# Norm scales applied at the eviction from PSUM instead of before the matmul, in a layer of retention, spatial gating and MLP

## The reference, cut to what matters

```python
def rmsnorm(x, g):
    y = x * lax.rsqrt(jnp.mean(x * x, axis=-1, keepdims=True) + EPS)
    return y * g
...
z = rmsnorm(x, g_mix) @ w_in                     # (B,S,3072)
q, k, v, g, u, sv = split(z)                     # 512 columns each
q = rotary(q); k = rotary(k) * 128 ** -0.5
r = layernorm_nogain(chunk_retention(q, k, v))   # over each head's 128 columns
y_ret = silu(g) * r * ret_norm_g
y_sg = spatial_gating(gelu(u), gelu(sv), w_s, b_s, sg_norm_g)
x = x + concatenate([y_ret, y_sg]) @ w_out
x = x + square(relu(rmsnorm(x, g_ffn) @ w_ff1)) @ w_ff2
x = x + sigmoid(rmsnorm(x, g_ple) @ w_ple_gate) * (p @ w_ple)
return rmsnorm(x, g_final)
```

## Time and profile before

| | us |
|---|---|
| median of 3 runs (lowest, highest) | 3551.35 (3355.66, 3689.61) |
| the profiled execution, device time | 3347.36 |
| its span on the slowest core (core 4) | 3345.5 |
| spans of the 8 cores | 3313.2 to 3345.5 |
| PE busy, core 4 | 3107.9 (93%) |
| DVE, ACT, POOL busy, core 4 | 1844.7, 1166.7, 547.4 |

### The profile page before, as it was taken

How to read it: one execution, slowest core, us unless ns; L and a number is a source line. 1 busy time by engine, 2 the same in 40 slices (tenths; PEclk the granted TensorE clock), 3 DMA queues, 4 the chain that set the end, 5 groups by cost and what they waited for, 6 DMA issues and landing times.

```text
span 3345.5 us, 45255 instructions; the slowest of 8 cores (3313.2 to 3345.5 us)
## 1 busy us (share of the span) xinstructions
PE 3107.9 (93%) x15322; PEld 1451.9 (43%) x15628; DVE 1844.7 (55%) x2864; ACT 1166.7 (35%) x2153; POOL 547.4 (16%) x512
## 2 busy tenths in 40 slices
PE   5999999889989899898999999999899999999996
PEld 2434444334434344344444444444444444444442
DVE  6756556555455454554546556465655555565426
ACT  5543344323323333233333323333333333333322
POOL 3401101202022120210202212021221202111000
PEclk9879999999999999999999999999999999999998
DMA  8856566444646447464464645536464464645442
GB/s 271 245 175 190 185 211 218 145 132 140 209 127 199 135 136 210 127 199 132 133 215 153 194 141 163 199 125 213 140 198 152 144 214 135 199 128 177 151 151 82
DMA packets 110689, 568.16 MB, mean 170 GB/s; under 512 B 19064, under 2 KB 19192, under 8 KB 60288
## 3 DMA queue, kind: packets, MB, share of 16 engines
q1 hardware_dynamic: 95488, 551.51, 50.6%
q10 hardware_dynamic: 14976, 13.74, 3.4%
HBM read 504.28 MB, written 60.92 MB: 169 GB/s over the span
## 4 chain that ended last, share of the span: by engine, by line
PE 75%; DMA 11%; DVE 8%; issue 3%; ACT 1%; POOL 1%; SPq 0%; DVEq 0%; ACTq 0%; POOLq 0%
PE ps L638 72%; DMA rsB<-rsd 7%; DVE TG L733 4%; DMA rsd<-st 4%; DVE xb L1112 1%; DMA xb<-wf 1%; ACT sq L669 1%; PE ps L646 1%; DVE xb L1050 1%; PE ps L999 0%; SPq L518 0%; POOL st L695 0%; DVE sq L674 0%; PE ps L848 0%; PE ps L878 0%
## 5 line engine op out<-in xcount | busy, mean ns | idle before, releaser
L638 PE MATMUL ps<-TG,ring 128*128 128x512 bf16 x7537 | 1759.3, 389 | 151.9 <-DVE TG L733 134.1
L638 PEld LDWEIGHTS ps<-TG,ring 128*128 128x128 bf16 x7680 | 758.3, 100 | 1076.7 <-issue 267.1
L638 PE MATMUL ps<-hT,ring 128*128 128x512 bf16 x3980 | 911.4, 380 | 8.4 <-ACT ring L602 1.6
L638 PEld LDWEIGHTS ps<-hT,ring 128*128 128x128 bf16 x4096 | 395.5, 98 | 460.6 <-issue 15.8
L1029 ACT ACTIVATE rel<-ps 128x512 f32<-128x512 f32 x512 | 304.0, 595 | 651.5 <-PE ps L638 584.9
L669 ACT ACTIVATE sq<-xb 128x1024 bf16<-128x1024 f32 x256 | 270.0, 1055 | 558.8 <-DVE xb L1050 191.9
L1031 DVE TENSOR_TENSOR hT<-rel 128x512 bf16<-128x512 f32 x326 | 245.2, 756 | 287.7 <-ACT rel L1029 287.6
L638 PE MATMUL ps<-ring,TG 128*128 128x512 bf16 x1502 | 361.7, 384 | 8.1 <-ACT ring L602 4.4
L733 DVE TENSOR_TENSOR TG<-xb,rsB 128x1024 bf16<-128x1024 f32 x191 | 226.6, 1248 | 210.9 <-DMA rsB<-rsd 205.6
L1050 DVE TENSOR_TENSOR xb<-xb,ps 128x512 f32<-128x512 f32 x288 | 192.8, 682 | 143.1 <-PE ps L638 125.9
L695 POOL TENSOR_TENSOR st<-st,NEGH 128x4 f32<-128x4 f32 x64 | 65.4, 1022 | 1209.6 <-DVE st L692 1209.6
(11 more groups left out here) (101 smaller groups left out, 2053.7 us busy)
## 6 DMA issues: line engine op xcount, KB each, us to landing
ring<-wb SPq DMA_DIRECT2D x366, 1024.0 KB, 6.0
xb<-wf SPq DMA_DIRECT2D x104, 512.0 KB, 8.3
xb<-xT SPq DMA_DIRECT2D x64, 512.0 KB, 9.1
out<-xb SPq DMA_DIRECT2D x64, 512.0 KB, 5.0
wb<-ring SPq DMA_DIRECT2D x26, 1024.0 KB, 9.8
rsB<-rsd ACTq DMA_DIRECT2D x52, 256.0 KB, 6.1
xb<-pT SPq DMA_DIRECT2D x16, 512.0 KB, 10.8
rot<-ROT SPq DMA_DIRECT2D x15, 512.0 KB, 7.9
```

The costliest lines, as they stand in the source:

```text
L638: r = e.matmul(out(), lhs(k), rhs(k), start=(start + k == 0), stop=(start + k == total - 1))
```

## The change

The matmuls no longer read a normalized residual, but a plain bf16 cast of it (`cast`: four casts of 128x1024, on ACT or DVE as the model picks). A norm's scale is one number per token, so it can be applied to the result. `norm` (the former `rstd`) computes it beside the matmuls:

- q and k are left without a scale. That of q is one factor per token of the retention's result and falls out in its layernorm, whose eps is scaled to match (`EPSQ`, L919 before); that of k moves to v, which is multiplied with the squared scale and the decay `KD` as it leaves PSUM (always DVE, a 128x16 table in `st`). `ktok` becomes a plain copy (DVE or ACT), and the table `DTm` is divided by KD.
- g: tanh with the scale as ACT's per-partition scale, and once more in the last product of the retention. sv: gelu with a per-partition scale.
- u and gate: one more DVE operation, PSUM times `rsB`, then ACT's gelu or tanh reads SBUF.
- `f_up`: one DVE operation, max(PSUM, 0) times `rsB`, in place of ACT's relu; the square is then on ACT or POOL, no longer on DVE.
- In every tile the scale is spread by PE, in three bf16 parts instead of two (two more small DVE operations, 12 rows instead of 8). The DMAs over DRAM and the tensor `rsd` are gone. In tiles 0 and 1, for the norms of mixer and MLP, PE also sums the squares directly, 8 one-column matmuls for each square, in place of DVE's additions.
- The model's numbers: completion delays, DMA bandwidth, durations; four `rsB` slots instead of two, seven `scr` instead of nine.
- The start: the pieces of tile 0 and of weight q are loaded alternately, tile 1 behind them, and the first `wb` writes later.

```diff
-SEM_LAT = {"pe": 0.25, "act": 0.12, "dve": 0.12, "pool": 0.15, "sp": 0.05}
+SEM_LAT = {"pe": 0.30, "act": 0.12, "dve": 0.19, "pool": 0.17, "sp": 0.05}
...
-            dma(lambda: rs_d[idx], lambda: stc(st, 4, 4), [(st, "rs")], [(dr, 0)], vt, lambda: ("rw", st.slot), 0, q="act")
-            dma(lambda: ap(rb), lambda: rs_d[idx].rearrange("(o p) b -> o (p b)", o=1).partition_broadcast(128).rearrange(
-                "p o n -> p (o n)"), [(dr, 0)], [(rb, 0)], vt, lambda: ("rb", rb.slot), 0, q="act")
...
-                f = lambda e, j=j: e.tensor_tensor(out=ap(dst)[:, 2 * j:2 * j + 2, :], in0=ap(X[t][j]),
-                                                   in1=r()[:, None, :].to_broadcast([128, 2, TT]), op=ALU.mult)
+        def cast(t, vt):
             dst = g.buf("TG")
             for j in range(4):
+                g.add(both(1024, lambda e, j=j: e.tensor_copy(out=ap(dst)[:, 2 * j:2 * j + 2, :], in_=ap(X[t][j])),
+                           lambda e, j=j: e.activation(out=ap(dst)[:, 2 * j:2 * j + 2, :], in_=ap(X[t][j]), func=AF.Copy)),
+                      [(X[t][j], 0), (X[t][j], 1)], [(dst, j)], vt, lock=("dve",))
...
-                g.add(both(512, lambda e, o=o, p=p: e.tensor_copy(out=ap(o), in_=ps(p)),
-                           lambda e, o=o, p=p: e.activation(out=ap(o), in_=ps(p), func=AF.Copy), mode=1),
-                      [(p, 0)], [(o, 0)], vt.v)
+                g.add({"dve": (T512, lambda e, o=o, p=p, b=b: e.tensor_tensor(
+                    out=ap(o).rearrange("p (h d) -> p h d", h=4), in0=ps(p).rearrange("p (h d) -> p h d", h=4),
+                    in1=stc(m.st, 16 + 4 * b, 4)[:, :, None].to_broadcast([128, 4, 128]), op=ALU.mult))},
+                      [(p, 0), (m.st, "r2")], [(o, 0)], vt.v)
...
-            g.add({"act": (t_act(512), lambda e: e.activation(out=ap(r), in_=ps(p), func=AF.Relu))},
-                  [(p, 0)], [(r, 0)], vt.v)
+            g.add({"dve": (T512 + .05, lambda e: e.scalar_tensor_tensor(out=ap(r), in0=ps(p), scalar=0.0, in1=ap(rb),
+                                                                       op0=ALU.max, op1=ALU.mult))},
+                  [(p, 0), (rb, 0)], [(r, 0)], vt.v)
+            g.add({"act": (t_act(512), lambda e: e.activation(out=ap(o), in_=ap(r), func=AF.Square)),
+                   "pool": (1.1, lambda e: e.tensor_tensor(out=ap(o), in0=ap(r), in1=ap(r), op=ALU.mult))},
+                  [(r, 0)], [(o, 0)], vt.v, lock=("pool",))
...
-                g.add({"act": (t_act(512), lambda e, p=p, gt=gt: e.activation(out=ap(gt), in_=ps(p), func=AF.Tanh,
-                                                                            scale=0.5))},
-                      [(p, 0)], [(gt, 0)], vt.v)
+                g.add({"dve": (T512, lambda e, p=p, gt=gt: e.tensor_tensor(out=ap(gt), in0=ps(p), in1=ap(rb), op=ALU.mult))},
+                      [(p, 0), (rb, 0)], [(gt, 0)], vt.v)
+                g.add({"act": (t_act(512), lambda e, gt=gt: e.activation(out=ap(gt), in_=ap(gt), func=AF.Tanh, scale=0.5))},
+                      [(gt, 0)], [(gt, 0)], vt.v)
```

More of the change, by code:

```diff
@@ L373, in _host_consts @@
     s = 128.0 ** -0.5
+    KD = np.stack([s * np.exp((127.0 - t) * lg[h]) for h in range(H)], axis=1)
     DTm = np.zeros((128, H, 128), np.float64)
@@ L396, in _host_consts @@
         ROT[tp, :, 1, :] = SW[:, tp * TT:(tp + 1) * TT]
-    SEL = np.zeros((8, NB, 128), f32)
-    for r in range(8):
+    SEL = np.zeros((12, NB, 128), f32)
+    for r in range(12):
         SEL[r, r % NB, :] = 1.0
@@ L416, in t_act @@
     return 0.19 + n / 1200.0
-T512 = 0.70
+T512 = 0.62
+A512P = 0.69
 P512 = 1.29
@@ L515, in csc, with dma @@
             return cs[:, i:i + n]
-        def dma(out, in_, reads, writes, vt, key, nbytes, q="sp"):
-            g.add({q: (0.1, lambda e: e.dma_start(out=out(), in_=in_()))}, reads, writes, vt, dma=key, nbytes=nbytes)
+        def dma(out, in_, reads, writes, vt, key, nbytes, q="sp", margin=0.0):
+            g.add({q: (0.1, lambda e: e.dma_start(out=out(), in_=in_()))}, reads, writes, vt, dma=key, nbytes=nbytes,
+                  margin=margin)
         def cload(name, dst, src, vt, nbytes=65536):
@@ L563, in unit_scale, with load_unit @@
             return None
-        def load_unit(name, vt, wbvt=30.0):
+        def load_unit(name, vt, wbvt=30.0, late=0.0):
             ring = "ring"
@@ L663, in load_x, with norm @@
                     [(X[t][j], 0), (X[t][j], 1)], vt + 0.01 * j, lambda b=X[t][j]: ("xl", b.slot), 524288)
-        def rstd(t, which, vt, on_pe):
+        def norm(t, which, vt):
+            p, st = g.buf("psum"), g.buf("st")
             acc = None
@@ L670, in rstd, with psums @@
                       [(X[t][j], 0), (X[t][j], 1)], [(s, 0)], vt)
-                if acc is None:
+                if t < 2 and which < 2:
+                    def psums(e, a=s, j=j):
+                        r = None
+                        for k in range(2):
+                            for b in range(NB):
+                                r = e.matmul(ps(p)[:, b:b + 1], ap(a)[:, k, b * 128:(b + 1) * 128], ones[:, :],
+                                             start=(j == 0 and k == 0 and b == 0), stop=(j == 3 and k == 1 and b == NB - 1))
+                        return r
+                    g.add({"pe": (0.45, psums)}, [(s, 0), c("ones")], [(p, 0)], vt)
+                elif acc is None:
                     acc = s
@@ new lines, in norm @@
+            g.add({"dve": (TINY, lambda e: e.tensor_tensor(out=ap(hl)[:, 8:12], in0=stc(st, 8, 4), in1=ap(hl)[:, 4:8],
+                                                          op=ALU.subtract))},
+                  [(st, "d"), (hl, 1)], [(hl, 2)], vt)
+            g.add({"pe": (0.1, lambda e: e.matmul(ps(p1)[0:12, 0:128], ap(hl), ident[:, :], start=True, stop=True))},
+                  [(hl, 0), (hl, 1), (hl, 2), c("ident")], [(p1, 0)], vt)
+            g.add({"dve": (0.3, lambda e: e.tensor_copy(out=T["rT"][:, rT.slot], in_=ps(p1)[0:12, 0:128]))},
+                  [(p1, 0)], [(rT, 0)], vt)
@@ new lines, in bc @@
+            def bc(e):
+                r = None
+                for b in range(NB):
+                    bs = slice(b * 128, (b + 1) * 128)
+                    r = e.matmul(ps(p2)[:, bs], sel[:, bs], T["rT"][:, rT.slot], start=True, stop=True)
+                return r
+            g.add({"pe": (4 * MS, bc)}, [(rT, 0), c("sel")], [(p2, 0)], vt)
+            rb = g.buf("rsB")
+            g.add({"act": (t_act(512), lambda e: e.activation(out=ap(rb), in_=ps(p2), func=AF.Copy))},
+                  [(p2, 0)], [(rb, 0)], vt)
@@ L758, in m_prep @@
             load_x(t, vx)
-            m.n1 = normed(t, 0, vn, t in ON_PE)
+            m.n1 = cast(t, vn)
+            m.st, m.rb = norm(t, 0, vn)
             m.A1 = [(m.n1, j) for j in range(4)]
@@ L1086, in gate @@
                   lock=("dve",))
-            n3 = normed(t, 2, v0 - 10, t in ON_PE)
+            n3 = cast(t, v0 - 10)
+            rb = norm(t, 2, v0 - 10)[1]
             A3 = [(n3, j) for j in range(4)]
```

186 lines of the change are left out of this document (81 added, 105 removed).

## The result

The changed kernel takes 3172.68 us in the median of 4 runs (3170.94 to 3279.89), the kernel before 3453.51 in 4 runs beside it (3353.03 to 3689.61). The ratio is 0.9457, with an interval of 0.9429 to 0.9484, so it is 5.4% faster. The ratio compares only runs in which no die ran at the lowered clock, which both kernels meet now and then (the 3279.89 is such a run). The profiled execution took 3171.47 us against 3347.36 before, and its span is 175.6 us shorter. The forecast was 3215.

A forecast was written before the change was run, and what follows sets the result against it. PE, busy 93% of the span, bounds the kernel, idling mostly for TG. Sum: 3347.4 - 128 + 5 - 34 + 20 + 15 + 5 - 10 - 3 = 3217, said as 3215 us; range 3150 to 3430.

The forecast's parts named there:

- TG's wait: PE's 134.1 us of waits for TG, the normalized residual, go except 5.95 at the start: -128 us, with +5 left.
- The clock behind the waits: PE's first matmuls after each long TG wait run at the lower clock level; that loss goes: -34 us.
- 372 more PE instructions: Small spreading and one-column sum matmuls added to PE, at about 0.055 to 0.06 us each: +20 us, bounds 20 and 87.
- The chain of small steps: In every norm PE's list waits for small steps between squares' sums and spread scale: +15 us, bounds 0 and 56.
- Evictions on DVE: DVE takes over PSUM evictions in `f_up` and gate, ending near 1,900 us busy, not the bound: +5 us, bound 50.
- ACT's queue: Fewer DMAs on ACT's queue; its idle time is off the path, so nothing beyond the gain from TG's wait.
- The start: First transfers reordered: PE begins near 10 us, q and k end near 56 instead of 64: -10 us, bounds 0 and -20.
- The end: The last gates' TG wait goes, but the last norm has two more steps: -3 us, bounds +10 and -10.
- the first (DVE or the small chain stalls PE): Rival: PE waits for DVE's PSUM evictions or the norms' small steps instead; time 3260 to 3380, chance 0.12.
- The third (the change doesn't do what it says): Rival: waits for the cast or for weights replace the 134 us; time near 3330, chance 0.05.
- The second: Rival: a longer stretch of lowered clock; 3300 us for 500 us of it, 3414 and more beyond 1,130; chance 0.17.
- the prediction's last case: The lowered clock holds to the kernel's end, as the Trainium skill's page would have it: 3840 us, chance 0.02.

## Why the prediction was right, and where its sizes were not

Direction and mechanism held. Of the terms, the first held; the second and third were both too small and nearly cancel; the fourth was far too large. Step by step:

1. **TG's wait (-128, with 5 left).** Right. In the middle 124.6 us of it went, 9.5 more before it, and nothing is left for the cast. What I had not counted is the 14.4 us row for the spatial gating's `v`, 8 waits that I had passed over as small. It hung on the same round trip (it comes back in the kernel with cast and DRAM) and went too.
2. **The clock behind the waits (-34).** The balance of the middle bears it out but doesn't measure it alone: 144.5 us shorter, of which waits 134.7 (142.6 - 7.9); PE's new instructions cost 33 (next step); so some 43 us are left for the clock behind waits. The forecast had added up only the 15 waits of over 3.5 us. The granted clock from 550 to 3000 us is 1.00, where the kernel before had 0.97, long after the lowered stretch of the earlier trace rows. Its row of that window:

```profile
550.00:3000.00 2450.00, 2302.05 (x11445) 1080.36 (x11673) 1340.21 (x2050) 811.66 (x1519) 410.31 (x385) 0.97 0.53 166
```

3. **372 more PE instructions (+20).** Too small. 250 of them lie in the middle (50 norms that DRAM had spread), and at the 0.13 us of the experiment with the scale over DRAM they cost 33 us; the price of those at the start wasn't taken apart. The reading of the earlier trace rows was wrong: 48 spreading matmuls are busy for 5.2 us there, which is 0.43 us for four, not 0.22. So steps 2 and 3 were off by some 9 and 13 us in opposite directions, and that their sum came out within 4 us is luck.
4. **The chain of small steps (+15).** Oversized. In the middle PE of core 7 waited 5.0 us for the parts, once, and never for `rT`; the timeline above shows 2.3 and 0.9 us to spare, as the count of covering matmuls in the order had said. I had allowed for a DVE that is late, and it wasn't.
5. **Evictions on DVE (+5).** Nothing, not even with 363 us more of them. DVE came to 1877.4 us (forecast about 1,900), ACT to 1233.2 (1,220). The evictions on their lines:

```profile
L1040 DVE SCALAR_TENSOR_TENSOR rel<-ps,rsB 128x512 f32<-128x512 f32 x512 | 352.3, 689 | 303.8 <-PE ps L639 297.7 <-PE ps L1009 1.5 <-POOL scr L807 1.0
```

   Of the 303.8 us that DVE idled ahead of them, 297.7 ended with PE's matmuls: DVE waits for PE, not the other way round.

6. **ACT's queue (0).** Nothing to see, and nothing was expected.
7. **The start (-10).** The start came to -25.7, and early transfers are not what made it so. PE does begin early, as its timeline on core 7 shows (the counterpart of the earlier trace rows):

```profile
9.80 0.35 PE L678 MATMUL ps<-ones,sq 128*128 128x1 bf16 x8 [9.80 <-ACT sq L671]
10.58 3.37 PE L639 MATMUL ps<-TG,ring 128*128 128x512 bf16 x8 [0.42 <-ACT ring L603]
...
56.42 3.57 PE L639 MATMUL ps<-TG,ring 128*128 128x512 bf16 x8 [5.04 <-DVE scr L813]
...
67.71 3.10 PE L639 MATMUL ps<-TG,ring 128*128 128x512 bf16 x8 [3.42 <-ACT scr L805]
70.60 1.76 PE L639 MATMUL ps<-ring,TG 128*128 128x512 bf16 x5
```

   But q and k don't end at 56: the last of them wait for rotations (`scr`, L805 and L813) to free their banks, v begins at 70.60, and the first transposes of q and k come at 84.9 us, where the cores of the kernel before had them at 84.8 (core 4) to 86.8 (core 2). PE beginning 14 us earlier was worth nothing on this core. In the mean of the cores the transposes come at 82.1 us, and with the old order of the transfers at 82.7. The 25.7 us up to the first `f_down` matmul have other sources. 16 are the lowered-clock stretch of the earlier trace rows, which core 4 had in the profiled execution and which die 0 hadn't (its cores were at this matmul at 217.5 to 219.6 us, die 1's at 235.7 to 237.1). I had carried that stretch over into the forecast as if it belonged to the kernel; it belonged to the execution. Of the other 10, 1.9 lie before the transposes and 7.7 behind them: from there core 2 of the kernel before needed 132.8 us to this matmul, core 7 of the changed one 125.1. A wait of 4.1 us for the third tile's TG (at 186.19) is among them, and a granted clock of 0.97 against 1.00 (some 4 us); nothing tests this split. The experiments do say where it doesn't come from: the first `f_down` matmul begins at 218.8 us, in the mean of the cores, with the spreading alone, but at 207.3 with the changed kernel's cast and the old order of transfers, at 207.0 with the old numbers and at 206.4 with the scale over DRAM. So it comes with what these kernels have in common, the cast and what belongs to it (in tiles 0 and 1 also PE's direct sums), and not with the transfers, the numbers or the spreading, as far as each was undone by itself.
8. **The end (-3).** -5.4. It too is in the cast and what belongs to it: the spreading alone has 70.0 to 71.2 us there, the changed kernel 64.3 to 65.4.

The sum by the terms: the middle was forecast at -117 and came to -144.5. The allowances of steps 1, 4 and 5 were 25 and 7.9 was needed (17 better), the overlooked row gave 14.4 and the small rows beside it 3.6; TG gave 3.4 less in the middle than counted, steps 2 and 3 together 4 less. The start came to -25.7 instead of -10, the end was 2.4 better. That is the distance from 3217 to 3171.5. The step that failed by most is thus the allowance for DVE's lateness, 17 us, then the lowered clock carried over, 16, then the row left out, 14.4, then PE's new instructions, 13 us too cheap, and the clock behind waits, 9 us too small.

Of the rivals, the first (DVE or the small chain stalls PE) is excluded by the run with more DVE work. The third (the change doesn't do what it says) is excluded by the missing TG row. The second is in part open: the lowered clock occurs in single executions of every kernel here. One of the changed kernel's four timed runs, 3279.89, is one and lies 3.4% above the others. In the profiled execution, with PE busy for 97 or 98% of the span on all eight cores, the granted clock was 0.99 on both dies (0.991 to 0.994). The Trainium skill, TensorE: Matmul & The Clock Gate, Part 1: The HAM clock gate, would have it lowered for as long as the load lasts; this trace disagrees. Single executions come close to it on one die: one of the kernel with the moved multiplications took 3799.43 us, with a mean granted clock of 0.81 on the four cores of die 0 and 0.99 on die 1, and the prediction's last case was 3840. Whether a kernel with fewer pauses meets the lowered clock more often can be counted: a die had a mean granted clock below 0.95 in 13 of the 34 executions of the kernel before that ran beside the experiments, and in 20 of 53 of the changed kernel and its variants. That is 38% of each, so these runs show no such effect, though from one kernel to the next the share goes from 0 of 5 to 8 of 9.

**What the change's gain consists of.** Against the kernel before: landing time alone 2.6%, spreading on PE alone 4.0%, cast with the scale of three of four norms over DRAM 4.8%, all that the change does 5.4%. These don't add up (2.6 + 4.0 + 4.8 would be 11.4), because each removes the same 125 us of waiting by another way: a plan that knows of the delay, a shorter delay, or matmuls that don't need the result. The cast is the strongest since it takes the norm off PE's path altogether; the spreading then matters for `v` and a few waits for weights, and costs PE 24 us more than the DRAM way for three of four norms. With a plan that knows of the delay, the DRAM way had next to no waits either and was the faster one (3144.95 us).

## What to carry to other kernels

Where an engine that is the bound waits for a chain of small steps, ask first whether its instructions need the result at their start or only where they are evicted; a per-token factor can leave the matmul's input, and then the latency of the chain is hidden by order alone. Before rewriting, correct the planner's number for the slowest step (3.0 us stood for what took 5.2 and more), since that alone may give half. A stall read from one profiled execution may belong to the execution, not to the kernel: compare the other die before carrying it into a forecast, and sum the small rows of the list of waits too, by what they hang on. Take the waits out of two times before dividing their difference by a count of instructions, too: with them left in, the 12.2 us above would have made a small matmul half as dear as it is.
